# Expert gates of a routed feed-forward layer: one-hot matmuls or an indirect accumulating scatter

## What is computed

```python
v1, i1 = lax.top_k(s1, 16)            # per token and head, 128 row keys
v2, i2 = lax.top_k(s2, 16)            # 128 column keys
cs, ci = lax.top_k(cand, 16)          # 16 of the 256 sums of pairs
experts = row * 128 + col             # 8 heads x 16 experts for each of 256 tokens
gates = jax.nn.softmax(cs, axis=-1)
a = jax.nn.gelu(einsum('chkd,cd->chk', expert_u[ec], hc))
w = gc * a
out = einsum('chk,chkd->cd', w, expert_v[ec])
```

## Time and profile before

| | |
|---|---|
| median of 3 runs | 3443.43 us (3442.79 to 3451.92) |
| span of the profiled execution | 3442.4 us |
| PE (TensorE) busy | 3212.0 us, 93% |
| DVE (VectorE) busy | 1998.8 us, 58% |
| ACT (ScalarE) busy | 1469.0 us, 43% |
| POOL busy | 60.3 us, 2% |
| mean DMA rate | 172 GB/s |

### The profile page before, as it was taken

The page is one execution under the profiler, slowest core; times in us unless marked ns, Lnnn a source line. Parts: engine busy times, 40 slices in busy tenths (PEclk is TensorE's granted clock), DMA queues, the critical chain, the costliest instruction groups (busy, mean ns, idle before and its releaser), DMA issues.

```text
span 3442.4 us, 49676 instructions
## 1 busy us (share of the span) xinstructions
PE 3212.0 (93%) x17240; PEld 2720.7 (79%) x17240; DVE 1998.8 (58%) x3069; ACT 1469.0 (43%) x1846; POOL 60.3 (2%) x109
## 2 busy tenths in 40 slices
PE   7999989889999999999369999999799999899998
PEld 6877767667999999999358888888577877687776
DVE  4466666545688666664654445445546565448554
ACT  3334443343444566664124444444433343434333
POOL 0000000000000000000000000000000000000000
PEclk9999999999999999999689999999899999899659
DMA  6554343445455555555645555555545455455104
GB/s 215 190 188 161 141 141 141 151 169 177 161 184 183 179 196 199 196 199 188 219 165 186 187 188 189 187 186 188 195 173 188 159 183 173 139 190 183 50 23 167
DMA packets 160299, 591.67 MB, mean 172 GB/s; under 512 B 18080, under 2 KB 18128, under 8 KB 158144
## 3 DMA queue, kind: packets, MB, share of 16 engines
q1 hardware_dynamic: 147600, 535.89, 44.7%
q0 software_dynamic: 12592, 54.31, 4.2%
HBM read 569.15 MB, written 20.97 MB: 171 GB/s over the span
## 4 chain that ended last, share of the span: by engine, by line
PE 77%; DVE 6%; ACT 2%; DMA 2%; issue 1%; DVEq 0%; POOL 0%; ACTq 0%; SPq 0%
PE bank L486 10%; PE bank L488 9%; PE bank L487 9%; PE bank L645 7%; PE bank L646 7%; PE bank L647 7%; PE bank L699 7%; PE bank L700 7%; PE bank L701 7%; PE bank L521 2%; PE bank L661 2%; PE bank L455 1%; DMA xt_hi<-gates_scratch 1%; DVE hall L1516 1%; DVE lo L1084 1%; PE bank L533 1%
## 5 line engine op out<-in xcount | busy, mean ns | idle before, releaser
L1084 DVE TENSOR_TENSOR lo<-raw,hi 128x1024 fp32r<-128x1024 f32 (+1 forms) x1025 | 1252.1, 1222 | 1256.4 <-ACT hi L804 1243.0
L804 ACT ACTIVATE hi<-raw 128x1024 fp32r<-128x1024 f32 (+1 forms) x1025 | 1083.8, 1057 | 1612.9 <-PE bank L488 895.1
L486 PE MATMUL bank<-hi,xt_hi 128*128 128x512 f32 (+1 forms) x2052 | 821.7, 400 | 29.4 <-DVE lo L1084 14.5
L488 PE MATMUL bank<-hi,xt_lo 128*128 128x512 f32 (+1 forms) x2052 | 803.0, 391 | 0.0
L487 PE MATMUL bank<-lo,xt_hi 128*128 128x512 f32 (+1 forms) x2052 | 801.7, 391 | 0.0
L645 PE MATMUL bank<-xt_hi,hi 128*128 128x256 f32 x2048 | 590.9, 289 | 2.2 <-DVE gate_t L1489 1.5
L646 PE MATMUL bank<-xt_lo,hi 128*128 128x256 f32 x2048 | 579.9, 283 | 0.0
L647 PE MATMUL bank<-xt_hi,lo 128*128 128x256 f32 x2048 | 579.7, 283 | 0.0
L486 PEld LDWEIGHTS bank<-hi,xt_hi 128*128 128x128 f32 x2052 | 387.2, 189 | 163.8 <-DVE lo L1084 48.1
L699 PE MATMUL bank<-hi,w_hi 128*128 128x512 f32 x1024 | 406.3, 397 | 85.5 <-DVE w_lo L1528 82.5
L488 PEld LDWEIGHTS bank<-hi,xt_lo 128*128 128x128 f32 x2052 | 387.2, 189 | 84.9
(11 more groups left out here) (179 smaller groups left out, 1877.1 us busy)
## 6 DMA issues: line engine op xcount, KB each, us to landing
raw<-in_w_u SPq DMA_DIRECT2D x256, 512.0 KB, 3.5
raw<-in_w_v SPq DMA_DIRECT2D x256, 512.0 KB, 3.4
raw<-in_w_ein SPq DMA_DIRECT2D x128, 512.0 KB, 3.5
raw<-in_w_oin SPq DMA_DIRECT2D x72, 512.0 KB, 3.4
raw<-in_w_att SPq DMA_DIRECT2D x64, 512.0 KB, 3.5
raw<-in_w_gate SPq DMA_DIRECT2D x64, 512.0 KB, 3.4
raw<-in_w_out SPq DMA_DIRECT2D x32, 512.0 KB, 3.4
raw<-in_w_qp SPq DMA_DIRECT2D x32, 512.0 KB, 3.5
```

Of the source, the lines that this page charges most:

```text
L486: pe.matmul(acc, xh, h_[:, s], start=first, stop=False)
L488: mm = pe.matmul(acc, xl, h_[:, s], start=False, stop=last)
L804: act.activation(hi[d][:, 0:width], raw[s][:, 0:width], ACT.Copy).then_inc(hi_ready, 1)
L1084: dve.tensor_tensor(lo[d][:, 0:width], raw[s][:, 0:width], hi[d][:, 0:width].bitcast(F32), ALU.subtract)\
```

## The change

It drops the one-hot tables, TensorE's products, the turning of ROW, COL and GATE, the stage of copies and the saves. Instead POOL fills `gates_scratch` with zeros early in the program, VectorE works out for each choice the flat address in that tensor (column x 32768 + row x 256 + token), and POOL adds each gate to its cell with indirect DMAs, one for each of the 256 columns of [128 tokens x 256 choices]; between heads it waits for all that are under way. The tensor is now laid out by tile. The gate multiply moves into the V stage, per tile, from groups of four tiles; nine slots hold them (one of its own, eight in `xt`). The U accumulators move to banks 6 and 7, V's first tile waits for the last GELU only at its last quarter, and VectorE's V stage is written out without a loop.

On POOL, early in the program, and then in place of the saves and the loads:

```diff
+            gp.memset(zero[:, :], 0.0).then_inc(zero_ready, 1)
+            gp.wait_ge(zero_ready, 1)
+            for c in range(4):
+                gp.dma_start(gates_dram[16 * c:16 * c + 16].rearrange("a p c -> p a c"),
+                             zero[:, :].unsqueeze(1).to_broadcast([P, 16, 512])).then_inc(gates_zeroed, 16)
             gp.wait_ge(region_free, freed.next())
             row("b_gate", B_GATE, 2)
...
-            with gp.Fori(0, GATE_TILES // 2) as i:
-                for g in range(2):
-                    gp.wait_ge(gates_staged, i * 2 + (g + 3))
-                    gp.dma_start(gates_dram[i * 2 + g], STAGE[:, g]).then_inc(gates_saved[g], 16)
...
-            gp.wait_ge(block_used, FIRST["w_v"])
-            for c in range(8):
-                if c >= 2:
-                    gp.wait_ge(gates_used, c - 1)
-                gp.dma_start(GATES_BACK[c % 2], gates_dram[8 * c:8 * c + 8].rearrange("g p n -> p g n"))\
-                  .then_inc(gates_back[c % 2], 16)
+            gp.wait_ge(gates_zeroed, 4 * 16)
+            gp.wait_ge(routed, 1)
+            cells = gates_dram.rearrange("a p (c one) -> (a p c) one", one=1)
+            for h in range(H):
+                if h:
+                    gp.wait_ge(scattered, 16 * 2 * TOPK * h)
+                for t in range(2):
+                    for k in range(TOPK):
+                        c = t * P + h * TOPK + k
+                        gp.indirect_dma_start(cells, bass.IndirectOffsetOnAxis(ap=place[:, c:c + 1], axis=0),
+                                              picked[:, c:c + 1], None, compute_op=ALU.add).then_inc(scattered, 16)
+            gp.wait_ge(scattered, 16 * 2 * TOPK * H)
+
+            tiles = gates_dram.rearrange("a p c -> (a p c)").rearrange("(j p t) -> p j t", j=N_EXPERT_TILES, p=P)
+            for n in range(N_EXPERT_TILES // GATE_GROUP):
+                if n == 1:
+                    gp.wait_ge(block_used, FIRST["w_v"])
+                if n > GATE_SLOTS:
+                    gp.wait_ge(gated, GATE_GROUP * (n - GATE_SLOTS + 1))
+                gp.dma_start(GATE_IN[gate_slot(n)], tiles[:, GATE_GROUP * n:GATE_GROUP * n + GATE_GROUP])\
+                  .then_inc(gates_in[gate_slot(n)], 16)
```

On TensorE, in `expert_u` and `expert_v`:

```diff
-                        acc = bank[2 * (g % 2)][:, 0:T]
+                        acc = bank[6 + g % 2][:, 0:T]
-                        if gates is not None and kk == 3:
-                            gates(2 * (j % 2) + q, i)
+                        if first and q == 1 and t == 1:
+                            pe.wait_ge(chunk_out, FIRST_CHUNK["w_u"] + N_EXPERT_TILES)
```

On ScalarE, in `high_weights`:

```diff
+                    act.wait_ge(gated, i * 2 + (j + 1))
```

On VectorE, after the gates are normalised, and then in the V stage:

```diff
+            done(dve.tensor_tensor(PICK_P, ident[:, :], iota[:, :], ALU.mult))
+            done(dve.tensor_reduce(token[:, 0:1], PICK_P, AX.X, ALU.add))
+            done(dve.tensor_scalar(token[:, 1:2], token[:, 0:1], float(P), None, ALU.add))
+            for t in range(2):
+                ins = dve.tensor_scalar(place_f[:, t * P:t * P + P], ROW[:, t], float(T), token[:, t:t + 1], ALU.mult,
+                                        ALU.add)
+            done(ins)
+            done(dve.scalar_tensor_tensor(out=place_f[:, :], in0=flat(COL), scalar=float(P * T), in1=place_f[:, :],
+                                          op0=ALU.mult, op1=ALU.add))
+            dve.tensor_copy(picked[:, :], flat(GATE))
+            done(dve.tensor_copy(place[:, :], place_f[:, :]))
+            dve.sem_inc(routed, 1)
...
+            def gate(j):
+                n, g = divmod(j, GATE_GROUP)
+                if g == 0:
+                    dve.wait_ge(gates_in[gate_slot(n)], 16 * gate_round(n))
+                dve.wait_ge(chunk_out, FIRST_CHUNK["w_u"] + j + 1)
+                dve.tensor_tensor(GALL[:, j], GALL[:, j], GATE_IN[gate_slot(n)][:, g], ALU.mult).then_inc(gated, 1)
...
+            gate(0)
+            gate(1)
...
+            for j in range(N_EXPERT_TILES):
                 b = FIRST["w_v"] + 2 * j + 1
+                split(b)
+                if j + 1 < N_EXPERT_TILES:
+                    low_weights(j + 1, None)
+                if j + 2 < N_EXPERT_TILES:
+                    gate(j + 2)
+                split(b + 1)
```

More of the change, by code:

```diff
@@ L62 @@
 EVEN_ORDER = [0, 1, 2, 3, 4, 5, 10, 11, 12, 13, 8, 9, 14, 15, 6, 7]
-ROUTE_TILES, GATE_TILES = 48, 64
+ROUTE_TILES = 48
+GATE_GROUP, GATE_SLOTS = 4, 8
 FIRST_CHUNK = {}
@@ L103, in build @@
         iota16 = sb("iota16", 16)
[L104 to L108, removed]
+        place = sb("place", T, U32)
+        place_f = sb("place_f", T)
+        picked = sb("picked", T)
+        token = sb("token", 2)
+        zero = sb("zero", 512)
+        gate_first = sb("gate_first", GATE_GROUP * T)
         w_hi = [sb(f"w_hi{s}", T, F32R) for s in range(2)]
@@ L185, in build @@
         PICK = at(116, 128, 16)
+        PICK_P = at(116, 128)
         GS = at(124, 16)
         EXPG = at(125, 16, 16)
-        STAGE = at(124, 2, 512)
         GALL = at(0, N_EXPERT_TILES, T)
@@ L197, in build @@
         COS2, SIN2 = at(102, 2, 128), at(103, 2, 128)
-        GATES_BACK = [xt_hi_t[:, :].bitcast(F32).rearrange("p (g n) -> p g n", g=8),
-                      xt_lo_t[:, :].bitcast(F32).rearrange("p (g n) -> p g n", g=8)]
+        GATE_IN = [gate_first[:, :].rearrange("p (g t) -> p g t", g=GATE_GROUP)]
+        for xt in (xt_hi_t, xt_lo_t):
+            v = xt[:, :].bitcast(F32).rearrange("p (s g t) -> p s g t", s=GATE_SLOTS // 2, g=GATE_GROUP)
+            GATE_IN += [v[:, k] for k in range(GATE_SLOTS // 2)]
         ST = [at(104 + 1.5 * k, 384) for k in range(2)]
@@ L250, in build @@
         score_out = sem("score_out")
[L251 to L256, removed]
+        zero_ready = sem("zero_ready")
+        gates_zeroed = sem("gates_zeroed")
+        routed = sem("routed")
+        scattered = sem("scattered")
+        gates_in = [sem(f"gates_in{g}") for g in range(GATE_SLOTS + 1)]
         gated = sem("gated")
@@ L266, in build, with gate_slot, gate_round @@
         conv_hi = sem("conv_hi")
-        pair_mm = sem("pair_mm")
+        def gate_slot(n):
+            return 0 if n == 0 else 1 + (n - 1) % GATE_SLOTS
+        def gate_round(n):
+            return 1 if n == 0 else 1 + (n - 1) // GATE_SLOTS
         block = ctx.enter_context(nc.Block())
@@ L331, in _ @@
             load(iota16[:, :], a["iota"][:, 0:16], 4)
-            gp.sem_inc(stage_free, 2)
-            with gp.Fori(0, GATE_TILES // 2) as i:
-                for g in range(2):
-                    gp.wait_ge(gates_staged, i * 2 + (g + 3))
-                    gp.dma_start(gates_dram[i * 2 + g], STAGE[:, g]).then_inc(gates_saved[g], 16)
-                for g in range(2):
-                    gp.wait_ge(gates_saved[g], i * 16 + 16)
-                    gp.sem_inc(stage_free, 1)
-            gp.wait_ge(block_used, FIRST["w_v"])
-            for c in range(8):
-                if c >= 2:
-                    gp.wait_ge(gates_used, c - 1)
-                gp.dma_start(GATES_BACK[c % 2], gates_dram[8 * c:8 * c + 8].rearrange("g p n -> p g n"))\
-                  .then_inc(gates_back[c % 2], 16)
+            gp.wait_ge(gates_zeroed, 4 * 16)
[18 more added lines that the diff above has]
+                  .then_inc(gates_in[gate_slot(n)], 16)
             gp.wait_ge(x2_saved, 16)
@@ L425, in build @@
             "qp": [cols(QP, k) for k in range(16)],
-            "route": [cols(ROW, 0), cols(COL, 0), cols(GATE, 0)],
             "h3": [cols(H2, k) for k in range(16)],
@@ L631, in _, with expert_u @@
             pe.wait_ge(score_out, 8)
-            def expert_u(j, i, gates=None):
+            def expert_u(j, i):
                 g = FIRST_CHUNK["w_u"] + j
@@ L647, in expert_u @@
                         mm = pe.matmul(acc, l_[:, s], xt_hi[:, k], start=False, stop=k == 15)
-                        if gates is not None and kk == 3:
-                            gates(2 * (j % 2) + q, i)
                     mm.then_inc(block_used, 1)
[L652 to L662, removed]
             for j in range(ROUTE_TILES):
                 expert_u(j, None)
[L666 to L671, removed]
-                for j in range(2):
[L673 to L679, removed]
+            with pe.Fori(0, (N_EXPERT_TILES - ROUTE_TILES) // 2) as i:
+                for j in range(2):
+                    expert_u(ROUTE_TILES + j, i)
             def expert_v(j, i, first, last):
@@ L942, in gelu @@
                 dst = GALL[:, j] if i is None else GALL[:, bass.ds(i * 2 + j, 1)].rearrange("p a t -> p (a t)")
-                act.activation(dst, bank[2 * (g % 2)][:, 0:T], ACT.Gelu_apprx_tanh).then_inc(chunk_out, 1)
+                act.activation(dst, bank[6 + g % 2][:, 0:T], ACT.Gelu_apprx_tanh).then_inc(chunk_out, 1)
             def tile_u(j, i=None):
@@ L957, in _ @@
                .then_inc(act_out, 1)
[L958 to L961, removed]
+            tile_u(ROUTE_TILES)
+            act.wait_ge(routed, 1)
+            tile_u(ROUTE_TILES + 1)
```

(27 more changed lines are left out.)

## The result

The change makes the kernel slower: 3514.98 us median (3514.15 to 3517.47), against 3447.07 before on the same chip; the ratio is 1.02, with a 95% interval of 1.0185 to 1.0215, so the loss is clear of the noise. I had forecast 3313 us, a gain of 4%, and a range up to 3450.

A forecast was written before the change was run, and what follows sets the result against it. TensorE, busy 93% of the span, was taken as the bound, with one 82.5 us hole before V. Gains of 140.3 us less 10 lost took 3442.4 to 3312.1, with the median's 1.0 3313 us; range 3298 to 3450.

The forecast's parts named there:

- Item 7: Scatter on POOL during U: 256 indirect DMAs at 1.3 us each, hidden in a 456 us window; +5 us for stream slips.
- rival (b): Scatter late but cheaper than the hole it replaces: 1.66 to 2.17 us each, 3400 us in all; chance 0.11.
- Rival (a): In U, splits held up by scatters, priced at 33 us, with blocks taking 3.1 us; chance 0.12.
- items 1 and 2: In U: dropping the one-hot products gains 55.8 us, and less loss around the routing gains 1.5 us.
- Rival (d): Gain given back: per-tile multiply or late groups delay V, zeros cost more, scatter late; about 3441 us; chance 0.03.
- Rival (c): DMA engines become the bound through the scatter's 4-byte pieces: V starts 394 us late, 3707 us; chance 0.16.
- Item 3: Transition from U to V: wait 1.8 us instead of 82.5, gaining 80.7, plus 2.3 us from no clock drop.
- Item 4 and 6: V stage: per-tile gate multiply hidden behind w_lo, costing nothing; loading 4.2 MB of gates as V begins, +2 us.
- Item 5: Program start: zeroing 16.8 MB by four DMAs on POOL's queue beside the weight stream, +3 us, bounds 0 and 11.

The follow-up runs named there:

- e1: The change, with VectorE's split in the 80 U tiles after routing subtracting from a PSUM bank, so reading SBUF once; 3372.68 us, ratio to before 0.9778.
- e7: The change with splits halved, zeroing moved into the gate stage, and each head's scatters waiting only for the same tokens' scatters of the head before; 3345.55 us.
- e5: The change, with each VectorE split of the 80 U tiles after routing written as two 128x512 instructions; 3386.31 us, ratio to before 0.9821.
- e4: The change, scattering only heads 0 to 3 (128 of 256 scatters), the other gates left out; 3322.8 us, ratio to before 0.9636.

## Why the prediction was wrong

- **Item 7, the scatter, is the step that failed,** twice over. I took 1.3 us for each, between 0.54 and 3.9, and measured is 1.54 plus 0.30 between two, so 1.85. That alone is over the 1.66 us at which I had the scatters just hidden; it leaves a wait of 48 us (e1), which is still a gain. And beside the splits it is 2.88, over the 2.17 us at which rival (b) ends, where by my sum the gain is gone ((2.17 - 1.66) x 256 = 130 us). That is the mechanism that sank it: the item gave the scatter a price of its own, and no price for waiting on VectorE. The window (456 us) was right: the trace gives the last start of a U matmul 459.8 us after the first scatter. The seven waits between heads were right as well, 3.7 us each (e7) where I had 3.9.
- **Rival (a) had the right mechanism and the wrong victim.** I priced only splits held up by a scatter (33 us). None was: splits last 1.22 us as ever, and U takes 741.1 us against the 741.5 that items 1 and 2 give (798.8 less 57.3). The scatter waits for the split. It costs the scatter the rest of the split each time, and as 1.54 + 0.30 us is a little more than the 1.65 us that a split leaves free in a block, it locks in step with the block. Worked out from my own rows, 256 x 2.878 = 737 us, it would have given a slower kernel; I left that side out. I also used the even 540 to 547 ns of the plain saves as evidence against it, though I had noted that they need not show it. They could not have: by the timeline of the kernel before, none of the 64 saves begins while a split runs. In the change one plain load of V does, 0.02 us into a split, and takes its usual time:

```profile
2144.12 1.23 DVE L1067 TENSOR_TENSOR lo<-raw,hi 128x1024 fp32r<-128x1024 f32 x1 [0.92 <-ACT hi L798]
...
2144.14 0.75 POOL L366 DMA_DIRECT2D xt_lo<-gates_scratch  x1 [22.38 <-DVE hall L1220]
```

The Trainium skill (SBUF — State Buffer, Who interferes with whom) says that a VectorE instruction with two SBUF inputs contends with a GpSimd instruction that reads SBUF, and that whoever is first makes the other wait for the whole instruction; this is the section that the prediction meant. For a scatter that comes second the traces agree: 2.58 us beside two inputs (after), 1.54 to 1.57 beside one (e1, but for one of 1.66), and 1.75 beside a half (e5). For a split that comes second they do not show it: one that begins 0.33 us after a scatter (at 1173.98 in the change) takes 1.23 us like all others.

- **Rival (b)** had the form of the result, a late scatter with VectorE's first multiply waiting for the gates, but a price of 1.66 to 2.17 us and no reason for it. On average it was 2.50 (641 us over 256). **Rival (d)** did not come: the multiply and the loads gave back 1.5 us in V.
- **Rival (c), the DMA engines, is out.** POOL's queue (q0) took 10.2% of 390 us for 19501 packets, 0.033 us each. Item 7 had 0.035 from the earlier trace rows, where its own terms, 0.647 less 0.616, give 0.031.
- **Items 1 and 2** (products and routing): -57.7 us measured, -57.3 predicted, for the two together.
- **Item 3** (transition): e4 shows 1.2 us of wait and no slow clock, predicted 1.8. In the change the long wait brought the slow first block back (granted clock 0.73).
- **Item 4 and 6** (multiply in V, loads): V without its half-clock loss is 1.5 us longer in e4; predicted 2.
- **Item 5** (zeros): 7.4 us; predicted 3, with a bound of 11. The argument that 2 KB rows yield to the stream was too kind: POOL's queue, which carries the zeros, took 71.8% of the engines from 14 to 86 us, and the weights' queue only 30.1%.
- **The rest of the early loss,** 12 us, is no step of mine: a slow first attention in that execution, with the stages about it. The profiled execution of the kernel before had a quick one, so the two profiles set the change some 12 us too far back.

With the measured 1.85 us or half the scatters the sum of items comes out within 0.4%: e1 3372.68 against 3313 + (1.85 - 1.66) x 256 = 3362, e4 3322.8 against 3313.

## What to carry to other kernels

When work moves to a queue that no row of the profile shows, its price in place is the question: compute the pace at which it is just hidden and the pace at which the gain is gone, and ask which engine's instructions stand beside it all the time. An indirect DMA of 128 elements costs POOL 1.85 us here, and when it begins inside a split, which reads two inputs from SBUF, it waits for the split's end; a stream of such splits whose gaps are a little too short turns that into one DMA per gap. Cutting the split in two took TensorE's wait from 189.8 to 65.3 us, of the 48.0 that are left without the lock, for 0.06 us a block on VectorE. A row is evidence against contention only if the two instructions overlap in it in the order that is feared; look before using it. Start such a queue from the first half of its input rather than from the whole.

## What was not expected of the hardware

- The lock step: 2.58 + 0.30 = 2.88 us is the length of a block to the hundredth, and 133 of the 162 scatters in U went by it.
- The waiting goes one way in these traces: scatters waited for splits, and no split in the change got longer than 1.23 us.
- Accumulating pieces of 4 bytes in HBM cost the DMA engines 0.033 us each, about what a small packet of the plain saves comes to (0.031, from the earlier trace rows).
- The first attention ran 20.6 to 20.7 us in some executions and 28 to 30 in others, with a granted clock of 0.57 to 0.81 over stretches of 20 us in it.
